# Entry loads with a semaphore each, a 16-column border band, and a normalisation moved between two weight roundings

## The reference

```python
h = layer_norm(x, P['ln0_g'], P['ln0_b'])            # entry, width 1024
z = h @ P['w_in'][l]                                  # 1024 -> N_IN columns
qa, ka, va, ub, vb, xc, qkv, zg, bd, ad = jnp.split(z, idx, axis=-1)
# gated branch (256 wide, 4 groups of 64)
u = jax.nn.gelu(ub)
vn = layer_norm(jax.nn.gelu(vb).reshape(b, t, G_B, DG_B), ln_g, ln_b)
mixed = jnp.einsum('gts,bnsgd->bntgd', w, vn...)      # inside chunks of 128 tokens
ob = u * mixed
# pooling branch: mean over the last 2, 4, 8 or 16 tokens minus the token itself, one window per group of 64
d = means - xc
oc = jnp.einsum('btgc,gcd->btgd', d, w_pool) * gamma
...                                                   # attention, delta rule, cross-attention, experts
```

## Time and profile before

| | |
|---|---|
| median of three runs | 1592.48 us |
| lowest, highest | 1586.08, 1593.78 us |
| the profiled execution, whole | 1597.02 us |
| its span (first to last instruction) | 1595.2 us |
| mean granted TensorE clock | 0.928 of full |
| PE busy | 1381.3 us, 87% of the span, 9942 records |
| DVE busy | 645.6 us, 40% |
| ACT busy | 550.7 us, 35% |
| POOL busy | 159.7 us, 10% |

### The profile page before, as it was taken

How to read it: one execution, slowest core, us unless ns; L and a number is a source line. 1 busy time by engine, 2 the same in 40 slices (tenths; PEclk the granted TensorE clock), 3 DMA queues, 4 the chain that set the end, 5 groups by cost and what they waited for, 6 DMA issues and landing times. The chain is left out here.

```text
span 1595.2 us, 25519 instructions
## 1 busy us (share of the span) xinstructions
PE 1381.3 (87%) x9942; PEld 963.9 (60%) x9943; DVE 645.6 (40%) x1025; ACT 550.7 (35%) x1072; POOL 159.7 (10%) x154
## 2 busy tenths in 40 slices
PE   4998999689999889888997997989982799998980
PEld 2444999665567777776886996767862333332320
DVE  4331555248732223445773002328546233322226
ACT  1222323258752633434212213423220333342425
POOL 0000000003320132210000000000000122321210
PEclk9999999879999878999998998999985899999995
DMA  9111121114004310003104106515243588897336
GB/s 331 44 56 40 30 61 40 49 56 159 1 20 142 102 47 16 3 3 122 60 40 145 40 16 226 227 60 197 85 165 152 210 265 265 269 299 231 77 60 227
DMA packets 83684, 185.03 MB, mean 116 GB/s; under 512 B 12948, under 2 KB 48923, under 8 KB 77171
## 3 DMA queue, kind: packets, MB, share of 16 engines
q1 hardware_dynamic: 76523, 157.14, 27.5%
q0 software_dynamic: 6912, 25.17, 6.7%
q10 hardware_dynamic: 144, 1.25, 0.2%
HBM read 144.31 MB, written 39.31 MB: 115 GB/s over the span
## 5 line engine op out<-in xcount | busy, mean ns | idle before, releaser
L3104 PE MATMUL bank<-arena,hT 128*64 x384 | 178.3, 608 | 9.9 <-DVE hT L3220 5.6
L3104 PEld LDWEIGHTS bank<-arena,hT 128*64 128x64 f32 x384 | 51.5, 140 | 112.2 <-issue 109.4
L479 PE MATMUL bank<-arena,hT 128*128 128x512 f32 x256 | 112.6, 598 | 0.0
L2176 PE MATMUL bank<-hT_rest,f_w_high 128*128 128x352 f32 x288 | 93.2, 324 | 0.0
L3107 PE MATMUL bank<-arena,hT 128*64 128x512 f32 x192 | 91.3, 621 | 0.0
L3130 PE MATMUL bank<-arena,hT 128*64 x192 | 87.5, 598 | 0.7 <-ACT hT L3171 0.7
L3107 PE MATMUL bank<-h,hT 128*64 128x512 f32 x192 | 87.0, 596 | 0.0
L479 PEld LDWEIGHTS bank<-arena,hT 128*128 128x128 f32 x256 | 48.6, 193 | 58.3 <-issue 58.2
L3060 POOL DMA_INDIRECT expert_sums<-hT,row_slot x24 | 48.2, 2010 | 222.4 <-DVE hT L3226 161.4
L2175 PE MATMUL bank<-hT_high,q_w_high 128*128 128x352 f32 x192 | 62.7, 326 | 4.0 <-DVE q_w_low L2468 4.0
L2175 PE MATMUL bank<-f_h_high_a,f_w_high 128*128 128x352 f32 x180 | 59.0, 328 | 6.7 <-DVE f_w_low L689 6.7
(11 more groups left out here) (501 smaller groups left out, 3163.9 us busy)
## 6 DMA issues: line engine op xcount, KB each, us to landing
arena<-in_ex_wg_dram SPq DMA_DIRECT2D x16, 1024.0 KB, 5.0
arena<-in_ex_wu_dram SPq DMA_DIRECT2D x16, 1024.0 KB, 8.4
arena<-in_ex_wd_dram SPq DMA_DIRECT2D x16, 1024.0 KB, 12.1
tokens<-h SPq DMA_DIRECT2D x24, 512.0 KB, 2.6
arena<-in_cache_mem_k_dram SPq DMA_DIRECT2D x8, 1024.0 KB, 4.9
arena<-in_w_in_dram SPq DMA_DIRECT2D x12, 512.0 KB, 4.0
h<-tokens SPq DMA_DIRECT2D x6, 1024.0 KB, 7.6
h<-in_x_prompt_dram SPq DMA_DIRECT2D x8, 512.0 KB, 8.8
```

The costliest lines, as they stand in the source:

```text
L479: last = nc.tensor.matmul(ps[bank][0:r, 0:n], hT[:, k, i * P:i * P + r], wt[:, k, col:col + n], start=(k == 0), stop=(k == KC - 1))
L2176: nc.tensor.matmul(out, high, w_low, start=False, stop=False)
L3104: nc.tensor.matmul(ps[UPB[u % 2]][rows_of(0), :], xT[:, u % 2, k, rows_of(0)], gate_up_of[:, bass.ds(slot, 1), :, k, :].rearrange("p a g f ...
```

## The change

Three parts.

1. Entry. The loads of `x` get four semaphores (tile 0, tile 1, tiles 2 and 3, tiles 4 to 8), and the three weight pieces and the identity block get one each. SP's order becomes: tile 0, `g`, `b`, key/value weights, tile 1, gate/pool weights, tiles 2 and 3, the other 18 blocks of constants, tiles 4 to 8, the eight narrow columns. ACT loads the identity alone. PE turns tile i+1 between the two halves of project(i) instead of ahead of them, and waits for each weight piece where it first reads it. ACT copies tile 0 before it takes the deviation of tile 1.
2. Features. The deviation of the gated values (table load, Ln, Exp) moves in ACT's list from behind group 11 to behind group 2, and the three scaling passes in DVE's list from behind `low_w(11)` to between `low_w(10)` and `low_w(11)`.
3. Gate and pool. The product with `bandprev` covers 16 columns of the output instead of 128.

```diff
-    x_in = [s(f"e_x{n}") for n in range(3)]
+    x_in = [s(f"e_x{n}") for n in range(4)]
+    x_group = lambda i: (0, 1, 2, 2, 3, 3, 3, 3, 3)[i]
+    x_count = lambda i: 16 * (1, 1, 2, 5)[x_group(i)]
...
             for i in range(TILES):
-                sp.dma_start(h[0:rows(i), i, :], x_tile(T, i)).then_inc(x_in[min(i // 2, 2)], 16)
+                sp.dma_start(h[0:rows(i), i, :], x_tile(T, i)).then_inc(x_in[x_group(i)], 16)
                 if i == 0:
                     sp.dma_start(g, row_bc(T['ln0_g'])).then_inc(ln_in, 16)
                     sp.dma_start(b, row_bc(T['ln0_b'])).then_inc(ln_in, 16)
+                    sp.dma_start(wt[:, :, 0:512], w_view[:, :, KA:KA + 512]).then_inc(w_kv, 16)
                 if i == 1:
-                    sp.dma_start(wt[:, :, 0:512], w_view[:, :, KA:KA + 512]).then_inc(w_in, 16)
-                    sp.dma_start(wt[:, :, 512:1024], w_view[:, :, VB:VB + 512]).then_inc(w_in, 16)
-                    sp.dma_start(wt[:, :, 1024:1032], w_view[:, :, BD:BD + 8]).then_inc(w_in, 16)
+                    sp.dma_start(wt[:, :, 512:1024], w_view[:, :, VB:VB + 512]).then_inc(w_vx, 16)
+                if i == 3:
+                    sp.dma_start(c.const[:, P:], T['const_tables'][:, P:]).then_inc(const_in, 16)
+            sp.dma_start(wt[:, :, 1024:1032], w_view[:, :, BD:BD + 8]).then_inc(w_ba, 16)
...
-            act.dma_start(c.const[:, :], T['const_tables']).then_inc(const_in, 16)
+            act.dma_start(c.const[:, 0:P], T['const_tables'][:, 0:P]).then_inc(ident_in, 16)
...
-                    if i + 1 < TILES:
+                    if 1 <= i < TILES - 1:
                         deviation(i + 1)
                     for q in range(2):
                         ...
+                    if i == 0:
+                        deviation(1)
...
             def project(i):
                 pe.wait_ge(hT_ok, 2 * i + 2)
+                if i == 0:
+                    pe.wait_ge(w_kv, 16)
...
                     last.then_inc(out_sem, 1)
+                    if col == 0:
+                        turn(i + 1)
+                        if i == 0:
+                            pe.wait_ge(w_vx, 16)
...
             turn(0)
-            pe.wait_ge(w_in, 48)
             for i in range(TILES):
-                if i + 1 < TILES:
-                    turn(i + 1)
                 project(i)
                 if i >= 1:
                     turn_k(i - 1)
...
+                if n == 2:
+                    nc.scalar.preload_act_table_set(EXPLN)
+                    act.wait_ge(stats, 1)
+                    link(nc.scalar.activation(mom[:, 1, :], mom[:, 1, :], ACT.Ln, bias=c.eps, scale=1.0 / DH))
+                    nc.scalar.activation(mom[:, 1, :], mom[:, 1, :], ACT.Exp, scale=-0.5).then_inc(rstd_ok, 1)
                 if n >= 4:
                     if n - 4 < 6:
                         conv_silu(n - 4)
-            nc.scalar.preload_act_table_set(EXPLN)
-            act.wait_ge(stats, 1)
-            link(nc.scalar.activation(mom[:, 1, :], mom[:, 1, :], ACT.Ln, bias=c.eps, scale=1.0 / DH))
-            nc.scalar.activation(mom[:, 1, :], mom[:, 1, :], ACT.Exp, scale=-0.5).then_inc(rstd_ok, 1)
...
-            for n in range(10, len(plan)):
-                low_w(n)
+            low_w(10)
             dve.wait_ge(rstd_ok, 1)
             ...
                                     ALU.add).then_inc(normed, 1)
+            low_w(11)
...
-                        last = nc.tensor.matmul(out, xc[:, i - 1, g * DH:(g + 1) * DH], band(f"bandprev{g}"),
-                                                start=False, stop=True)
+                        last = nc.tensor.matmul(out[:, 0:POOLB + 1], xc[:, i - 1, g * DH:(g + 1) * DH],
+                                                band(f"bandprev{g}", P, POOLB + 1), start=False, stop=True)
```

More of the change, by code:

```diff
@@ L324, in stage_entry @@
     s = c.sem
-    x_in = [s(f"e_x{n}") for n in range(3)]
+    x_in = [s(f"e_x{n}") for n in range(4)]
+    x_group = lambda i: (0, 1, 2, 2, 3, 3, 3, 3, 3)[i]
+    x_count = lambda i: 16 * (1, 1, 2, 5)[x_group(i)]
     h_out = s("e_h")
-    w_in, const_in, ln_in = s("e_w"), s("e_const"), s("e_ln")
+    w_kv, w_vx, w_ba, ident_in, const_in, ln_in = s("e_wkv"), s("e_wvx"), s("e_wba"), s("e_ident"), s("e_const"), s("e_ln")
     eps_set, stats, rstd_ok, normed = s("e_eps"), s("e_stats"), s("e_rstd"), s("e_normed")
@@ L374, in _ @@
             for i in range(TILES):
-                dve.wait_ge(x_in[min(i // 2, 2)], 32 if i < 4 else 16 * (TILES - 4))
+                dve.wait_ge(x_in[x_group(i)], x_count(i))
                 if i >= 2:
@@ L448, in _ @@
         def _(pe):
-            pe.wait_ge(const_in, 16)
+            pe.wait_ge(ident_in, 16)
             def turn(i):
@@ L501, in _ @@
             pe.wait_ge(pad_ok, 1)
+            pe.wait_ge(w_ba, 16)
+            pe.wait_ge(const_in, 16)
             for n in range(GRP):
```

## The result

| | before | changed |
|---|---|---|
| median | 1593.13 us (1586.08 to 1597.20, 4 runs) | 1569.18 us (1567.71 to 1571.38, 4 runs) |
| profiled execution | 1597.02 us | 1567.71 us |
| its span | 1595.2 us | 1565.9 us |

The ratio is 0.9851 [0.9826, 0.9877], a gain of 23.7 us [19.6, 27.7] of 1593. The forecast was 1571 us and a gain of 21.7. Faster, and inside the range. The ratios here are taken over executions in the usual, fast state, which leaves out two that no profile explains: one of `after_bands` at 6790.51 us and one of the kernel before, timed beside `both_18`, at 2414.48 us.

What follows compares the result with a forecast made beforehand. PE, 87% busy, bounds the kernel, so edits pay where it idles or its work shrinks. Gains of 10.4 + 11.3 + 0 = 21.7 us from 1592.48 give 1570.8, said as 1571 us; range 1563 to 1581.

Steps and rivals of the forecast that it cites:

- Entry: Entry stage: first product moves from 24.99 to 13.7 us, one turn of 0.87 comes back; gain 10.4 us.
- the slow beginning stays ... 1.3 us: Entry, first project: it took 15.22 us against 13.90, and these 1.3 us were left as they are.
- upper bound of 11.6: Entry: if `b` came at about 6.4 us, the weights' 12.5 would bind and the gain be 11.6 us.
- Tail: End of features stage: PE starts the next stage at 302.67 instead of 314.01 us; gain 11.3 us.
- cover of 3.8 us: Features: the three moved DVE passes end at 281.3 us, 3.8 us ahead of the start of `low_w(11)`.
- Border band: Gate stage: 28 products shrink from 128 to 16 columns; weights set the pace, so gain 0 us.
- Clock at the gate's start: Start of the gate stage: the granted clock falls to 0.50 once more.
- the rival said it stays up: Gate stage's start: the 0.8 us gap leaves the clock at 2.4 GHz, saving about 2.0 us; 1569 us, 15%.
- DMA less early: Entry: something other than bytes limits the loads, so part 1 gains 7.1 us; 1574 us, 15%.
- Small products dearer: Gate stage: the 16-column border products cost 3.9 us more instead of nothing; 1575 us, 10%.
- Tail not won: Features' end: the store or a late last rounding holds the block, leaving only part 1; 1582 us, 9%.
- A stall in each turn: Entry: the turn inside project stalls PE in every tile; 6 us of stall each gives 1619 us, 3%.

Runs made afterwards that it cites:

- after_bands: The changed kernel with the band matrices in five loads on three semaphores, those the first tile needs in front; median 1572.37 us.
- both_18: The changed kernel with band matrices in five loads and 18 unused identity products ahead of the first turn; median 1563.73 us, ratio 0.9803 to the kernel before.
- Warming: The changed kernel with 24 unused products of the identity with itself ahead of the first turn; median 1566.27 us.
- entry_only: The kernel before with only part 1 of the change; median 1582.06 us.
- entry_and_tail: The kernel before with parts 1 and 2, the border product left at 128 columns; median 1573.97 us.
- band_widths: The changed kernel with another width of the border product in each tile, 16 to 128 columns; 1568.3 us, one run.

## Why the prediction was right

**Entry: 10.4 said, 8.9 in this profile and 9.8 in the kernel with part 1 alone.** The steps came in their order, each somewhat late: `b` at 8.1 (7.4 said), the turn at 11.5 (10.9), the weights at 13.3 (12.5), the first product at 14.13 (13.7). That is 0.4 us of miss in the end. Tile 0 was late too (moments at 5.28, landing said for 4.1), which cost nothing, as `b` came later still. The larger one is the term "the slow beginning stays ... 1.3 us". Before, it was shared: two turns of 1.94 instead of 1.04, and 1.32 in the first project, 3.1 together. With tile 1's turn out of the way one turn carries 0.9, and the first half of the project pays the rest, 9.32 - 6.95 = 2.4. The slow beginning is fixed to PE's first work and falls on whatever stands there. Warming removed it, which shows it. Its length also varies: from the first product to the second turn it is 8.51 us in entry_only, 8.65 in entry_and_tail and 9.32 in the changed kernel, and this is nearly all of the difference between 9.8 and 8.9. The prediction's upper bound of 11.6 had a slip besides: with `b` at 6.4 the first product could start at 12.7, later than the weights, which gives 11.4.

**Tail: 11.3 said, 11.3 measured** (158.9 to 147.6, and PE's idle time at the boundary from 12.14 to 0.81, which doesn't depend on how long the stage itself took). The cover of 3.8 us was 3.51, the boundary 0.31 for 0.30.

**Border band: 0 said, 0.9 in the stage.** The failed step is "for 64 columns half of that, 0.06, is what the rows already show": that took the weights as the limit. The products of 128 columns were set by their columns, and the floor is half as high. Seven tiles at 0.25 us would be 1.7, a little over half of the upper bound of 3.1; the longer low clock took part of it back.

**Clock at the gate's start.** The prediction said 0.50 once more, leaning on the earlier trace rows; the rival said it stays up and 2.0 us are won. Neither held in the changed kernel's profile, though nothing was won, as forecast. The clock stayed at 1.00 for four us, as the Trainium skill has it (TensorE: Matmul & The Clock Gate, What's actually happening) for a gap so short, and here the trace agrees, with 0.81 us. But the time so won went into the wait for the band matrices, 2.44 us of idle time, and the clock was down before it ended. That wait is not what the fall needs: in after_bands and band_widths it came with no gap longer than 0.81, so there the traces do not agree with a low clock that returns only after an idle stretch. Only with the load split was there a gain, 3.7 us, and that at either clock.

The earlier trace rows was read wrongly. In the kernel before the gap at that boundary begins at 342.08, and the window ahead of it has the clock falling already, among small products:

```profile
340.00:342.00 2.00, 1.19 (x8) 0.97 (x8) 0.00 (x0) 0.77 (x3) 0.00 (x0) 0.92 0.00 0
```

So the 0.50 behind it says nothing about what a gap of 0.81 us does.

**The other rivals.** DMA less early: the landings were 0.7 and 0.8 us later than said, a fifth of the 3.3. Small products dearer: no. Tail not won: no. A stall in each turn: none, as the row of the 256 records shows. The entry behind the first product takes 132.0 us, against 130.1 before with 1.32 us of slow start; the difference is the turn of 0.87 and the dearer beginning of 1.1.

**Luck.** The entry gave 1.5 us less than said and the gate stage 0.9 more, so part of why the sum of 21.7 met the 21.1 is that two misses took each other back.

**What the sum missed** is not needed to explain the 23.7, since 21.1 lies inside [19.6, 27.7]. The two profiled executions alone would have given 29.3, and made a small error look large. What stays open is whether a kernel has odds of its own for the long delta stage, and what starts it.

## What to carry to other kernels

Give each load at the head of a kernel its own semaphore, order them by first use, count the bytes ahead of the one that is waited for, and then look at the order in the engine's list: the loads alone gave 3.0 us of 9.8. A serial tail at a stage's end belongs into idle time of the same engine before it; compare the pass lengths with the wait that is there. A faster piece ahead of a DMA wait gives nothing until the DMA comes earlier too: 12.96 us against 12.99 here.

## What the runs showed of the hardware that was not expected

- In the first 25 us the granted clock reads 1.00 in the windows, although TensorE is slow there: the weight loads of the first project in the changed kernel's timeline stand 0.85 us apart, and later 0.43. At the start of an execution the spacing tells the speed, not that column. The window and the weight loads:

```profile
14.00:16.00 2.00, 1.87 (x3) 0.84 (x4) 1.36 (x3) 0.08 (x1) 0.00 (x0) 1.00 1.05 410
```

```profile
15.15 0.33 PEld L487 LDWEIGHTS bank<-arena,hT 128*128 128x128 f32 x1 [0.52 <-issue]
16.00 0.33 PEld L487 LDWEIGHTS bank<-arena,hT 128*128 128x128 f32 x1 [0.52 <-issue]
...
19.59 0.19 PEld L487 LDWEIGHTS bank<-arena,hT 128*128 128x128 f32 x1 [0.24 <-issue]
20.02 0.19 PEld L487 LDWEIGHTS bank<-arena,hT 128*128 128x128 f32 x1 [0.24 <-issue]
```

- The granted clock can be 0.50 to 0.57 for 20 us with PE busy for 94% of them, and in other executions it is 1.00 and 0.83 at that place; the stage is about 7 us longer for it.
- At the gate stage's start it fell to 0.50 in some executions with no wait of PE longer than 0.81 us ahead, and in one (both_18) it stayed at 1.00 through a wait of 1.14.
- A product with 64 weight columns, in float32, gets hardly cheaper below 64 moving columns: 1.94, 1.94, 1.92 and 1.90 us per tile for 64, 48, 32 and 16.
- The head of the kernel with the table on the other queue delayed `b` by 3.0 us but not tile 0, whose moments began at 4.99 instead of 5.28. There the table was issued behind tile 0; in the kernel before, where it was issued beside it, tile 0 landed 6.6 us after its issue, and in the changed kernel 4.4.
